# Prelude of a two-block kernel: modulation products in four column groups between the first projection's blocks, scaled x in PSUM, another order of transfers, the last modulation rows later

## The reference

```
sh1x, sc1x, g1x, sh2x, sc2x, g2x = split(silu(c)     @ w_ada + b_ada, 6)   # 6 x 1024 columns
sh1c, sc1c, ...                  = split(silu(c_ctx) @ w_ada + b_ada, 6)
hc = rms_norm(ctx, norm1_g) * (1 + sc1c) + sh1c         # 256 context tokens
hx = rms_norm(x,   norm1_g) * (1 + sc1x) + sh1x         # 256 tokens of x
z  = hx @ w_in      # split into u, vs, q, r, ga, gb, k, v, lr
s_f, s_b = final states of a gated linear attention over hc (k, v, lr)
x = x + g1x * token_mixer(hx, s_f, s_b)
x = x + g2x * conv_ffn(rms_norm(x, norm2_g) * (1 + sc2x) + sh2x)
x = rms_norm(x, final_norm_g)
```

## Time and profile before

| | us |
|---|---|
| median of 3 runs | 1292.05 |
| lowest, highest | 1291.49, 1295.96 |
| profiled execution, its own time | 1294.34 |
| its span from first to last instruction | 1292.5 |
| TensorE busy in it | 1264.9 |
| mean granted TensorE clock in it | 0.989 of full |

### The profile page before, as it was taken

One profiled execution on the slowest core, in us unless ns is written; L12 is line 12 of the kernel. 1 busy time (PEld: TensorE's weight loads), 2 busy tenths in 40 slices (PEclk: granted clock), 3 DMA queues, 4 the chain that ended last, 5 costly groups with the idle time before them and its releaser, 6 DMA issues.

```text
span 1292.5 us, 27596 instructions
## 1 busy us (share of the span) xinstructions
PE 1264.9 (98%) x9770; PEld 1173.5 (91%) x9770; DVE 722.8 (56%) x1678; ACT 715.0 (55%) x1294; POOL 878.6 (68%) x386
## 2 busy tenths in 40 slices
PE   9999999999999999999999999999999999999997
PEld 3678899999988898898899989999999999999986
DVE  3989861132487772467465246555633766555633
ACT  3656644554666664486342247666655555666653
POOL 0447956578869889854233218888798787888795
PEclk9999999999999999999998899999999999999999
DMA  9985255345536555723222114555465554555562
GB/s 369 402 329 195 82 203 170 117 159 185 189 135 206 185 183 173 220 99 102 80 67 66 66 33 163 180 179 179 155 182 189 176 180 163 193 180 180 155 193 77
DMA packets 66025, 217.79 MB, mean 169 GB/s; under 512 B 9896, under 2 KB 17320, under 8 KB 62608
## 3 DMA queue, kind: packets, MB, share of 16 engines
q1 hardware_dynamic: 65936, 216.56, 49.5%
HBM read 215.48 MB, written 1.05 MB: 168 GB/s over the span
## 4 chain that ended last, share of the span: by engine, by line
PE 46%; issue 28%; POOL 22%; ACT 2%; DVE 2%; POOLq 0%; ACTq 0%; DVEq 0%
POOL w_lo L630 21%; PE bank L715 12%; PE bank L738 10%; PE bank L1071 5%; PE bank L744 5%; PE bank L830 4%; PE bank L747 2%; PE bank L839 2%; PE bank L834 1%; PE bank L1160 1%; DVE cbuf L2935 1%; PE bank L1137 1%; ACT w_hi L1614 0%; ACT h L1614 0%; PE bank L1107 0%
## 5 line engine op out<-in xcount | busy, mean ns | idle before, releaser
L630 POOL TENSOR_TENSOR w_lo<-w_raw,w_hi 128x1024 fp32r<-128x1024 f32 x340 | 814.6, 2407 | 375.9 <-ACT w_hi L1614 374.8
L1614 ACT ACTIVATE w_hi<-w_raw 128x1024 fp32r<-128x1024 f32 (+1 forms) x372 | 377.9, 1020 | 127.7 <-PE bank L839 37.9
L738 PE MATMUL bank<-a_hi,w_hi 128*128 128x264 f32 (+3 forms) x704 | 200.5, 285 | 0.1
L738 PE MATMUL bank<-a_hi,w_lo 128*128 128x264 f32 (+3 forms) x704 | 200.2, 284 | 0.0
L738 PE MATMUL bank<-a_lo,w_hi 128*128 128x264 f32 (+3 forms) x704 | 199.9, 284 | 0.0
L715 PE MATMUL bank<-a_parts,w_hi 128*128 128x256 f32 x960 | 173.8, 284 | 0.2
L715 PEld LDWEIGHTS bank<-a_parts,w_hi 128*128 128x128 f32 x960 | 149.7, 192 | 1.0 <-ACTq L1871 0.5
L715 PE MATMUL bank<-a_parts,w_lo 128*128 128x256 f32 x480 | 135.8, 283 | 0.0
L738 PEld LDWEIGHTS bank<-a_hi,w_hi 128*128 128x128 f32 x704 | 132.8, 189 | 0.4 <-DVE a_lo L3513 0.3
L738 PEld LDWEIGHTS bank<-a_lo,w_hi 128*128 128x128 f32 x704 | 132.9, 189 | 0.1
L738 PEld LDWEIGHTS bank<-a_hi,w_lo 128*128 128x128 f32 x704 | 132.9, 189 | 0.0
(11 more groups left out here) (507 smaller groups left out, 2813.9 us busy)
## 6 DMA issues: line engine op xcount, KB each, us to landing
w_raw<-in_s SPq DMA_DIRECT2D x284, 512.0 KB, 3.7
w_raw<-in_down SPq DMA_DIRECT2D x48, 512.0 KB, 3.5
adaw<-in_w_ada SPq DMA_DIRECT2D x16, 1024.0 KB, 10.7
w_raw<-in_down SPq DMA_DIRECT2D x24, 384.0 KB, 3.1
adab<-in_w_ada_first SPq DMA_DIRECT2D x8, 1024.0 KB, 8.9
ctxt<-in_ctx SPq DMA_DIRECT2D x1, 1024.0 KB, 11.3
x<-in_x SPq DMA_DIRECT2D x1, 1024.0 KB, 15.3
out_h<-h SPq DMA_DIRECT2D x4, 256.0 KB, 2.7
```

The source lines that it names most:

```text
L630: pool.tensor_tensor(w_lo[:, s], w_raw[:, s], w_hi[:, s].bitcast(F32), ALU.subtract) \
L738: ins = mm(banks[bank][:, tk], w_[:, s, k], x_[:, k, tk], start=(m == 0), stop=(m == 3 * KD - 1))
L1614: return nc.scalar.activation(out_, in_, f, **kw)
```

## The change

It does these things.

- Each modulation product's eight matmuls go to four groups of 32 columns: c_wide is c2 widened with zeros to 32 columns per k, the output of k goes to partitions 32(k % 4) of the bank. ACT copies all 128 partitions, and flip_rows becomes four matmuls by quarter_sum, which turn the rows and add the four quarters in one.
- The products stand between the blocks of w_k: product 0 before everything, product 1 after the first blocks of tiles 0 and 1, and so on. mean_square(ctx) and (x) come before product 0. 20 more warm-up matmuls, and eight after the first flip.
- x and ctx are scaled by gain and by 1/rms in one op each into PSUM (scaled_in(k)). ACT's a_hi and DVE's a_lo both take them from there and add the shift. xr goes.
- SP's order: ctx, x, averages and pv before the first product's weights; the units of w_k before product 1's weights; units 4 to 7 in one go, and of the modulation row pairs only 0, 1, 2 before unit 8.
- Pairs 12 to 15 of the modulation rows come in the stream of w_r to w_br_a, with c broadcast loaded a second time (csil_late) and silu made of it by ACT among w_r's tiles. DVE takes each in two ops of 1024 elements. The third norm's columns and g1 are ready as before, g2 (columns 40 to 48) later.
- DVE's list becomes modulations(0, 7), w2s, (7, 9), lrs, (9, 10), the adds behind the logits, (10, 11), decays, ..., (11, 12), and the last four between later work.

The diff, cut to its core:

```diff
-        ADA_RING = [5, 6, 0, 1, 2, 3, 4, 5, 6, 0, 1, 4, 0, 1, 4, 1]
+        ADA_RING = [5, 6, 0, 1, 2, 3, 4, 0, 1, 0, 1, 0, 7, 7, 7, 7]
+        EARLY_ROWS = 12
...
+        def scaled_in(k):
+            return banks[6 + k // 2 % 2 if k % 2 else 4]
...
 SP
-            for j in range(4):
+            def first_rows(j):
                 if j >= 2:
                     sp.wait_ge(ada_done, j - 1)
                 for half in range(2):
...
+            small(ctxt[:], a["ctx"], ctx_in)
+            small(x[:], a["x"], x_in)
+            small(averages[:], a["averages"], sums_in)
+            small(pv[:], a["pv"], sums_in)
+            first_rows(0)
             for s in range(SLOTS):
                 stream_unit("s0", s, s)
-            small(wlr[:], a["w_lr"], small_in)
-            small(csil[:], a["c"].partition_broadcast(P), small_in)
-            small(gla_masks[:], a["gla_masks"], small_in)
+            first_rows(1)
+            first_rows(2)
+            first_rows(3)
...
+                    small(wlr[:], a["w_lr"], small_in)
+                    small(csil[:], a["c"].partition_broadcast(P), small_in)
+                    small(gla_masks[:], a["gla_masks"], small_in)
+                    slot_units(4, 8)
                     ada_rows(0)
                     ada_rows(1)
...
+                    sp.wait_ge(std_ready, 2)
+                    ada_rows(2)
+                    slot_units(8, 9)
+                    ada_rows(3)
+                    slot_units(9, 10)
+                    sp.wait_ge(ada_done, 3)
+                    ada_rows(4)
+                    slot_units(10, 12)
+                    ada_rows(5)
+                    sp.wait_ge(ada_done, 4)
+                    ada_rows(6)
                     ada_rows(7)
+                    slot_units(12, 14)
                     ada_rows(8)
+                    slot_units(14, 16)
+                    for p in range(9, EARLY_ROWS):
                         ada_rows(p)
...
+                if u0 == 0:
+                    pieces = [(i, i + 2, 0) for i in range(first, n // 4, 2)]
...
+                    if u0 == 0 and at_ == 1:
+                        sp.wait_ge(sc_done, 4)
+                        sp.wait_ge(ks_ready, 2)
+                        sp.wait_ge(kt_done, 8)
+                        sp.dma_start(csil_late[:], a["c"].partition_broadcast(P)).then_inc(x_in, 16)
+                    if u0 == 0 and at_:
+                        ada_rows(EARLY_ROWS + at_ - 1)
...
+                if u0 == 0:
+                    ada_rows(15)
...
 TensorE
-            for _ in range(16):
+            for _ in range(36):
                 mm(banks[0][:, 0:P], part_sum[:, 0:P], part_sum[:, 0:P], start=True, stop=True)
...
                 if j >= 2:
                     pe.wait_ge(modrow_ready, j - 1)
+                    pe.wait_ge(split_ready, 8 * S_X + 2 * j - 2)
...
-                    ins = mm(banks[6 + j % 2][0:2, :], c2[:, k], adab[j % 2][:, k], start=(k == 0), stop=(k == KD - 1))
+                    q_ = 32 * (k % 4)
+                    ins = mm(banks[6 + j % 2][q_:q_ + 32, :], c_wide[:, k], adab[j % 2][:, k], start=(k < 4), stop=(k >= 4))
...
-                    ins = nc.tensor.transpose(banks[2 + j % 2][:, 2 * i:2 * i + 2],
-                                              modrow[:, j % 2, i * P:(i + 1) * P], ident[0:2, 0:2])
+                    ins = mm(banks[6 + j % 2][:, 2 * i:2 * i + 2], modrow[:, j % 2, i * P:(i + 1) * P], quarter_sum,
+                             start=True, stop=True)
...
+            mean_square(RMS_CTX)
+            mean_square(RMS_X)
             mod_rows(0)
-            mod_rows(1, 5, lambda: mean_square(RMS_CTX))
             flip_rows(0)
-            mod_rows(2, 1, lambda: mean_square(RMS_X))
+            fill(8)
+            def first_tiles(j, tiles):
+                for s in tiles:
+                    if j == 0:
+                        pe.wait_ge(lo_ready, s + 1)
+                        pe.wait_ge(banks_free, s + 1)
+                    ins = tile_blocks(s, 2 * j, 2 * j + 2)
+                    if j == 3:
+                        ins.then_inc(unit_used, 1)
+            first_tiles(0, (0, 1))
+            mod_rows(1)
+            first_tiles(0, (2,))
             flip_rows(1)
+            first_tiles(0, (3,))
+            mod_rows(2)
+            first_tiles(1, (0,))
+            flip_rows(2)
+            first_tiles(1, (1, 2))
             mod_rows(3)
+            first_tiles(1, (3,))
+            flip_rows(3)
+            first_tiles(2, range(SLOTS))
+            first_tiles(3, range(SLOTS))
...
 ACT
             root(RMS_CTX, N1, 0)
             root(RMS_X, N1, 0)
-            mod_rows(1)
-            modulated(0)
-            round_unit(0, 0)
-            mod_rows(2)
-            round_unit(1, 1)
-            modulated(1)
-            round_unit(2, 2)
-            mod_rows(3)
-            round_unit(3, 3)
+            mod_rows(0)
+            for s in range(SLOTS):
+                round_unit(s, s)
+            modulated(0)
+            mod_rows(1)
+            modulated(1)
+            mod_rows(2)
+            mod_rows(3)
             modulated(2)
             modulated(3)
...
-            units("w_r", evac_r, 0, 8)
+            units("w_r", evac_r, 0, 3)
+            act.wait_ge(x_in, 32)
+            fn(csil_late[:], csil_late[:], ACT.Silu).then_inc(csil_ready, 1)
+            units("w_r", evac_r, 3, 8)
...
 DVE
                 for k in (2 * j, 2 * j + 1):
-                    if k:
-                        dve.wait_ge(split_ready, 8 * S_X + k)
-                    for jj, src in enumerate((xr, ctxt)):
-                        ins = v.tensor_scalar(banks[4][:, jj * N1:(jj + 1) * N1], src[:, k], gain[:, jj, k:k + 1],
-                                              mod[:, jj, k:k + 1], ALU.mult, ALU.add)
+                    for jj, (src, r_) in enumerate(((x, r_x), (ctxt, r_ctx))):
+                        ins = v.scalar_tensor_tensor(scaled_in(k)[:, jj * N1:(jj + 1) * N1], src[:, k], gain[:, jj, k:k + 1], r_,
+                                                     ALU.mult, ALU.mult)
                     ins.then_inc(full_ready, 1)
...
+                for k in (2 * j, 2 * j + 1):
+                    dve.wait_ge(split_hi, 8 * S_X + k + 1)
+                    for jj in range(2):
+                        tk = slice(jj * N1, (jj + 1) * N1)
+                        ins = v.scalar_tensor_tensor(a_lo[:, k, tk], scaled_in(k)[:, tk], mod[:, jj, k:k + 1],
+                                                     a_hi[:, k, tk].bitcast(F32), ALU.add, ALU.subtract)
+                    ins.then_inc(split_ready, 1)
...
-            modulations(0, 9)
+            modulations(0, 7)
             dve.wait_ge(w2_ready, 1)
...
-            modulations(9, 10)
+            modulations(7, 9)
             dve.wait_ge(lr_hi, 1)
...
-            modulations(10, 11)
+            modulations(9, 10)
...
-            modulations(11, 15)
+            modulations(10, 11)
...
-            modulations(15, 16)
+            modulations(11, EARLY_ROWS)
```

More of the change, by code:

```diff
@@ L107, in bass_two_blocks @@
         over_d, over_dv, over_dh, ones = (averages[:, i] for i in range(4))
+        area_w = where[0]
         halves = sb("halves", [P, LOG2P - 1, P // 2])
+        c_wide = at("c_wide", [P, KD, 32], area_w)
         pairs_mask = sb("pairs_mask", [P, P], I32)
@@ L125, in bass_two_blocks @@
         mv = sb("mv", [P, 2, 4])
+        quarter_sum = stats[:, 0, 0, 0:2]
         area_x = where[0]
@@ L1682, in _ @@
             act.wait_ge(first_in, 32)
-            fn(c2[:], c2[:], ACT.Silu).then_inc(csil_ready, 1)
+            act.wait_ge(warm, 2)
+            fn(c_wide[:, :, 0:2], c2[:], ACT.Silu).then_inc(csil_ready, 1)
             nc.scalar.preload_act_table(ACT.Sqrt)
-            act.wait_ge(ctx_in, 48)
+            act.wait_ge(ctx_in, 16)
             for k in range(KD):
@@ L2587, in _ @@
                 two = slice(2 * j, 2 * j + 2)
-                v.tensor_tensor(ctxt[:, two], ctxt[:, two], lanes(r_ctx, 2), ALU.mult).then_inc(xr_ready, 1)
-                v.tensor_tensor(xr[:, two], x[:, two], lanes(r_x, 2), ALU.mult).then_inc(xr_ready, 1)
                 dve.wait_ge(mod_flipped, j + 1)
-                shift_, scale_ = (banks[2 + j % 2][:, 4 * part:4 * part + 4].rearrange("p (k j) -> p k j", j=2) for part in range(2))
+                shift_, scale_ = (banks[6 + j % 2][:, 4 * part:4 * part + 4].rearrange("p (k j) -> p k j", j=2) for part in range(2))
                 v.tensor_tensor(mod[:, :, two].rearrange("p j k -> p k j"), shift_, twice(b_ada[:, 0, two]), ALU.add)
@@ L2618, in modulations @@
                     dve.wait_ge(row_in[ring], 16 * ADA_RING[:p + 1].count(ring))
+                    if p >= EARLY_ROWS:
+                        dve.wait_ge(csil_ready, 4)
+                        for t in range(2):
+                            part = adaw[ring][:, t]
+                            ins = v.scalar_tensor_tensor(part, part, 1.0, csil_late[:], ALU.mult, ALU.mult,
```

(3 more changed lines are left out.)

108 lines of the change are left out of this document (37 added, 71 removed).

## The result

The changed kernel takes 1302.58 us (median of 5 runs, 1301.3 to 1303.32); the kernel before took 1291.49 us beside it (5 runs, 1289.38 to 1295.96). The ratio is 1.0076, interval 1.0056 to 1.0096. A second measurement, with 6 and 16 runs, gave 1302.57 against 1294.38 us, ratio 1.0061 [1.0041, 1.0081]. So the change costs 8 us by the larger sample, where 2.8 were forecast. Both medians lie 0.4 us under the upper end of the stated range of 1286 to 1303 us.

The account below looks back on a forecast made before the run. TensorE, busy 1264.9 of 1292.5 us, bounds the kernel; its list and the DMA bytes bound the prelude. An 8.8 us lead is lost waiting for late rows and pair 9 adds 2.8: profiled 1297.1, median 1294.9 us, range 1286 to 1303.

Parts of the forecast that it names:

- rival B: Modulation products: matmul records chain, 3.9 us each, w_k ends 7 us later at 62; +9, 1301 us; chance 0.18.
- The likeliest case: Whole kernel: late rows use up the lead before w_v's logits; +2.8 us, median 1294.9; chance 0.38.
- step 5: w_k: 96 matmuls 22 us, three products 5.2, three flips 1.5, waiting 2.2; end at 54.9 instead of 62.6 us.
- rival D: Prelude: TensorE's new pauses lower its clock, 3.2 us lost once or twice on top of +2.8; 1297 to 1301; chance 0.16.
- Step 1: Modulation products: four column groups run side by side, a product falls from 6.9 to 1.7 us.
- rival C: Modulation products: groups don't run side by side, 6.9 us each, w_k ends at about 70; +17, 1309 us; chance 0.08.
- Steps 2 to 4: Start of prelude: reordered transfers, w_k's first block at 24 instead of 40.04 us, scaled x in PSUM, TensorE leads.
- Steps 6 and 7: w_q to first logit: first rest 55.3 us, queues empty from 51.8, pair 8 lands 81.0, logit 84.2 against 84.72.
- Step 8: Logits: row pair 9 stands before the first bias add on DVE; third logit 89.4 instead of 86.63 us, +2.8.
- Step 9: After the logits: late row pairs, 2.5 us of DVE each, stay hidden; no time gained or lost.
- Rival A: Prelude: rows land in time, DVE alone bounds, pair 9 and the add done at 80.7 us; -5.9, 1286.2; chance 0.20.

Follow-up runs that it names:

- the second profile: Profile of the changed kernel timed once more, nothing edited: 1302.57 us (6 runs), ratio 1.0061 to the kernel before.
- The fillers before w_k: Changed kernel with 24 instead of 8 filler matmuls behind the first flip, before w_k's first block: 1299.69 us, ratio 1.0037 to the kernel before.
- both orders and product 1 first: Changed kernel, DVE row pairs 7-9 after logits' work, SP pairs 3-4 before unit 8, 20 fillers, product 1 before all w_k blocks: 1289.19 us, ratio 0.9971.
- DVE's order alone: Changed kernel with row pairs 7, 8 and 9 moved behind lrs and the adds in DVE's list, SP untouched: 1293.03 us, ratio 1.0002.
- fillers at the logit: Changed kernel with 30 unused filler matmuls on TensorE in the pause before the first logit: 1301.3 us, ratio 1.0057 to the kernel before.

## Why the prediction was right or wrong

The range held the result, by 0.4 us and with luck: its upper end had been set to take in rival B. The likeliest case did not hold. It was to be within 0.5% of before, in 1291 to 1299 us; both measured ratios lie above 1.005. The mechanism was the forecast one (rows late, the lead lost in one wait before the first logit), its size was not: 8 us instead of 2.8. The term that was too small is w_k's end in step 5 (54.9 us, measured 58.0 and 58.8), and the sum had no term for the slow clock behind TensorE's pauses, which stood in rival D alone.

- **Step 1, right.** 1.92 us a product against 1.7 taken; 7.8 us in all. The records chain (rival B) and groups that don't run side by side (rival C) are refuted by the group's row. The Trainium skill's figure for three column tiles ("TensorE: Matmul & The Clock Gate", "Measured speedup vs the span model") would have made it 2.9 us, an estimate; the rows show more, 28.2 / 7.8 = 3.6 times with four. C's own price was too low: its order took w_q to 78.2, not to 70, and the time to 1322, not to 1309.
- **Steps 2 to 4, right but for the pause.** First block at 24.95 against 24; four scaled x 0.39 apart, as taken.
- **Step 5, wrong by 3.1 to 3.9 us.** w_k was to end at 54.9; w_q starts at 58.01 and, in the second profile, at 58.81 us. With the pause filled it starts at 56.4. So 1.6 to 2.4 us are the clock, at half speed after the pause of 4.1 us, and 1.5 us are the sum's: 0.95 of a later first block, the rest in the list.
- **Steps 6 and 7, the mechanism right.** First rest of w_q forecast for 55.3, found at some 57.9 us (POOL starts it at 55.54). Gap of the queues forecast from 51.8 to 55.3, found from 52.5 to 57.5; pair 8 forecast to land at 81.0, DVE starts it at 84.19; first logit 84.2 against 87.48. These 3.2 us are those of step 5 passed on, since SP waits for w_q's first rest. The fillers before w_k show the link: 1.6 us at w_q, 1.9 at the first logit. The empty stretch of 30 to 33 us (SP waits for product 1 before it may issue the weights of product 3) was missed. I hold it for harmless, since the later gap would only have begun earlier. That wasn't tried on the changed kernel alone; with both orders and product 1 first it is filled, the later stretch eases instead, and no gain is seen.
- **Step 8, right in kind.** Third logit 89.4 forecast, 92.42 and 93.28 found, again by step 5. What I didn't see is how cheaply it is mended: three row pairs moved in DVE's list take back the 10 us at the third logit. The step had both waits and their cause before it.
- **Step 9, right that they are hidden, wrong in a size.** Nothing behind 93 us costs but the clock. The late pairs take DVE 4.1 us each (16.3 / 4), not 2.5, but TensorE is as busy with them as without.
- **Rival A** didn't come: the rows aren't in time, even with row pairs 3 and 4 sent ahead (third logit 90.15, where A had 80.7).
- **Rival D came, on top of the forecast.** It had 0.16 and a price of once or twice 3.2 us on top of the 2.8, 1297 to 1301 us (1298 to 1301 by its own sum); its sign, a clock below 1.00 before 100 us, stands in the trace. The clock takes 1.6 to 2.4 us before w_q and up to 2.0 behind the third logit, 4.4 of the 5.8 us by which the second profile's marker misses the forecast; nearly all of the rest is step 5's sum (1.5 us). The slow stretch of 84 to 91 us, behind the longest pause that D had named (8 us before the logit), costs nothing: it ends at the wait for DVE's add. The Trainium skill asks for no long idle gaps of TensorE between bursts ("TensorE: Matmul & The Clock Gate", "Why this matters for your kernels"), and the trace agrees: windows at 0.83 and 0.71 where there were pauses of 4.1 and 7.4 us, and 1.00 where they were filled. The price depends on what TensorE waits for next.

## What to carry to other kernels

When an engine's queue mixes work with a deadline (lrs, the adds) and work without one (the row pairs), write down for each item with a deadline what stands ahead of it and when that lands; transfers that land later can turn that list against the kernel, even when it has become shorter, and moving three row pairs gave back 10 us at the logits. Count a new pause of TensorE at more than its length: look at what runs at the lowered clock behind it and whether that leads straight to the end or into another wait. Judge a shift by a marker in the trace, and the time behind it by its share at half speed, before putting a few us down to an edit. And look where in the trace the work in question stands before choosing the stretch that is to show its price: the late rows lay ahead of the marker, not behind it.

## What the chip showed that I had not expected

- Four column groups of 32 run fully side by side in fp32 with 512 moving columns. The raw records of product 0 start at 15.304, 15.310, 15.317 and 15.324 us, the next four at 15.757, the next at 16.186: four records in the 0.43 us of one. Each record is about as long (608 ns) as without groups (594 ns).
- Pauses of TensorE of 4.1 and 7.4 us went with 3.4 to 13.7 us at half the clock (1.2 GHz), while the same places filled did not. Shorter ones did too: 2.76 us (DVE's order alone: half clock from 23.7 to 27.1 us) and 3.18 us (fillers at the logit: 93.7 to 97.1 us). After the 4.1 us pause the lowered stretch was 3.4 us in one execution of the changed kernel and 6.8 us in the other, after the 7.4 us pause 6.8 and 13.7 us: the same program, the same pauses.
- The late stretches add up to between 10.2 and 30.7 us in the thirteen executions of the table, worth up to 10 us of a span; less 0.49 us for each us of them, the rests behind the marker lie within 1.7 us of each other.
